# Ordering the second block's mixer steps by modelled engine times, with the convolution's taps as filler

## The reference

```python
z_conv, z_cq, z_ckv, z_kr, z_four = split_mixing(u @ w_in[l])
k_lat, v_lat = mla_kv(z_ckv, z_kr, ...)       # 8 heads, 64 + 32 wide keys, 64 wide values
q_lat = mla_q(z_cq, ...)
attn = attend_blocked(q_lat, concat(k_ctx, k_lat), concat(v_ctx, v_lat))
y = merge_branches(u, conv_module(z_conv, ...),  # 31 taps over time on 384 channels, layer norm, silu, w_pw
                   attn @ w_o_mla[l],
                   fourier_mix(z_four, ...),      # 4 groups: 2-D Fourier transform, then w_fourier
                   w_bgate[l], b_bgate[l], w_out[l])
# merge: (g0 * y_conv + g1 * y_mla + g2 * y_four) @ w_out, g = sigmoid(u @ w_bg + b)
```

## Time and profile before

| | |
|---|---|
| median of 3 runs | 2709.94 us (2701.28 to 2718.32) |
| profiled run: time, span | 2710.06 us, 2708.2 us |
| mean granted TensorE clock | 0.986 |
| TensorE busy | 2613.0 us (96%) |
| VectorE busy | 1691.8 us (62%) |
| ScalarE busy | 1084.0 us (40%) |
| HBM read | 377.40 MB, 140 GB/s |

### The profile page before, as it was taken

How to read it: one execution, slowest core, us unless ns; L and a number is a source line. 1 busy time by engine, 2 the same in 40 slices (tenths; PEclk the granted TensorE clock), 3 DMA queues, 4 the chain that set the end, 5 groups by cost and what they waited for, 6 DMA issues and landing times.

```text
span 2708.2 us, 38912 instructions
## 1 busy us (share of the span) xinstructions
PE 2613.0 (96%) x15924; PEld 2313.5 (85%) x15924; DVE 1691.8 (62%) x2681; ACT 1084.0 (40%) x1686; POOL 69.9 (3%) x64
## 2 busy tenths in 40 slices
PE   7999898999999999999999999999999999998998
PEld 7998788999888888778888888889888888888998
DVE  6767554677767655656644677655555456776664
ACT  5546633545322223344243422224222224555543
POOL 0001032000000000000010000000000000000000
PEclk9999899999999999999999999999999999999999
DMA  7764200566455543112323355543443433234454
GB/s 263 237 229 174 80 9 32 172 233 211 149 191 180 181 146 109 55 37 70 100 86 102 119 191 172 181 161 118 140 140 131 136 102 122 74 131 158 166 194 147
DMA packets 110114, 381.00 MB, mean 141 GB/s; under 512 B 12016, under 2 KB 17392, under 8 KB 109552
## 3 DMA queue, kind: packets, MB, share of 16 engines
q1 hardware_dynamic: 108928, 373.32, 41.3%
q10 hardware_dynamic: 1008, 5.18, 0.5%
HBM read 377.40 MB, written 1.05 MB: 140 GB/s over the span
## 4 chain that ended last, share of the span: by engine, by line
PE 88%; DVE 6%; ACT 4%; issue 2%; DMA 0%; ACTq 0%; DVEq 0%
PE B L1458 25%; PE B L1459 25%; PE B L1460 25%; ACT w_hi L1779 2%; DVE w_lo L2075 2%; PE B L1718 1%; PE B L1701 1%; PE B L1473 1%; PE B L1611 1%; PE B L1474 1%; PE B L1475 1%; PE B L1625 1%; PE B L1708 1%; PE B L1618 1%; DVE AC L2321 1%
## 5 line engine op out<-in xcount | busy, mean ns | idle before, releaser
L1458 PE MATMUL B<-U,w_hi 128*128 128x256 f32 (+1 forms) x2896 | 963.4, 333 | 9.5 <-DVE w_lo L2075 5.5
L1459 PE MATMUL B<-U,w_hi 128*128 128x256 f32 (+1 forms) x2896 | 953.9, 329 | 0.0
L1460 PE MATMUL B<-U,w_lo 128*128 128x256 f32 (+1 forms) x2896 | 953.7, 329 | 0.0
L2075 DVE TENSOR_TENSOR w_lo<-w_raw,w_hi 128x1024 fp32r<-128x1024 f32 (+3 forms) x587 | 684.6, 1178 | 418.1 <-ACT w_hi L1779 417.3
L1779 ACT ACTIVATE w_hi<-w_raw 128x1024 fp32r<-128x1024 f32 (+3 forms) x587 | 591.1, 1012 | 507.1 <-PE B L1460 484.1
L1458 PEld LDWEIGHTS B<-U,w_hi 128*128 128x128 f32 x2896 | 548.8, 189 | 66.5 <-issue 11.1
L1459 PEld LDWEIGHTS B<-U,w_hi 128*128 128x128 f32 x2896 | 547.1, 189 | 53.3 <-issue 2.2
L1460 PEld LDWEIGHTS B<-U,w_lo 128*128 128x128 f32 x2896 | 546.7, 189 | 51.5
L1458 PE MATMUL B<-HHf,w_hi 128*128 128x256 f32 (+1 forms) x1122 | 364.3, 325 | 1.8 <-DVE w_lo L2075 1.8
L1460 PE MATMUL B<-HHf,w_lo 128*128 128x256 f32 (+1 forms) x1122 | 363.6, 324 | 0.0
L1459 PE MATMUL B<-HLf,w_hi 128*128 128x256 f32 (+1 forms) x1122 | 363.6, 324 | 0.0
(11 more groups left out here) (351 smaller groups left out, 2628.9 us busy)
## 6 DMA issues: line engine op xcount, KB each, us to landing
w_raw<-in_w SPq DMA_DIRECT2D x504, 512.0 KB, 4.2
w_ada<-in_w SPq DMA_DIRECT2D x144, 512.0 KB, 3.4
w_raw<-in_w SPq DMA_DIRECT2D x58, 384.0 KB, 3.1
w_raw<-in_w SPq DMA_DIRECT2D x16, 240.0 KB, 2.5
X<-in_x SPq DMA_DIRECT2D x2, 1024.0 KB, 9.7
w_raw<-in_w SPq DMA_DIRECT2D x8, 256.0 KB, 2.7
BW<-in_bias ACTq DMA_DIRECT2D x1, 1536.0 KB, 10.2
K<-in_consts ACTq DMA_DIRECT2D x2, 640.0 KB, 5.7
```

The source lines that it names most:

```text
L1458: pe.matmul(o, hi, xh, start=i == 0 and s.start, stop=False)
L1459: pe.matmul(o, hi, xl, start=False, stop=False)
L1460: e = pe.matmul(o, lo, xh, start=False, stop=i == last and s.stop)
L2075: dve.tensor_tensor(w_lo[:, plan.slot[u], 0:n], w_raw[:, plan.ring[u], 0:n], w_hi[:, plan.slot[u], 0:n].bitcast(F32), ALU.subtract).then_i ...
```

## The change

`paced` gets three things: engine names in lower case take the engine's time but don't delay the task's own next step; a generator `spare` is drawn from while VectorE's clock is more than 150 ns behind TensorE's; and if nothing is due and nothing can start, time jumps ahead.

```diff
-def paced(tasks):
+def paced(tasks, spare=iter(())):
     free, later, ready = dict(P=0, A=0, D=0), list(tasks), {}
     while later or ready:
+        while free["D"] + HOP < free["P"] and (ns := next(spare, 0)):
+            free["D"] += ns
         for g in [*sorted((g for g in ready if ready[g] <= free["P"]), key=ready.get), *later]:
...
         else:
-            free["P"] = min(t for t in ready.values() if t > free["P"])
+            free["P"] = min([t for t in ready.values() if t > free["P"]], default=max(free.values()) + 1000)
             continue
...
             for engine, ns in took:
-                t = free[engine] = max(t, free[engine]) + ns
-                t += HOP
+                end = free[engine.upper()] = max(t, free[engine.upper()]) + ns
+                if engine.isupper():
+                    t = end + HOP
```

```diff
+        P = lambda k, n_=n: ("P", round(k * n_ * 1.328))
+        split = lambda c=1024: (("a", 150 + c), ("d", 150 + c))
+        A, Dv = (lambda n_=n, m=1: ("A", m * (200 + round(0.8 * n_)))), (lambda n_=n, m=1: ("D", m * (150 + round(1.05 * n_))))
         def taps():
-            left, turn = [(i, c) for i in range(1, 31) for c in range(3)], 0
-            while left:
-                turn += 1
-                k = pace[-1] * turn // 2 - pace[-1] * (turn - 1) // 2
-                self.add("taps", key=l, n=n, arg=tuple(left[:k]))
-                left = left[k:]
+            for i in range(1, 31):
+                for c in range(3):
+                    self.add("taps", key=l, n=n, arg=((i, c),))
+                    yield 180 + round(1.15 * n)
+            tapped.append(l)
+        def layer_norm():
+            while not tapped:
                 yield
...
latent:
-                yield
+                yield *split(), P(8, nn), ("d", 400 + 3 * nn), ("a", 400 + 2 * nn)
prep:
-                yield
+            yield *split(480), P(3), Dv(), P(2, 512), Dv(512)
...
+            yield ("P", 800 * ns), Dv(m=3)
soft:
-                yield
+            yield P(2, nk), Dv(nk), ("D", 150), Dv(nk), ("D", 150), A(nk), A(nk)
...
+            yield ("P", 275 * nk // 64), A(nk)
...
+            yield ("P", 140 * nk // 64),
...
fourier:
-                while not l and len(prepared) < 2 * j + 1:
-                    yield
...
+            yield *split(), P(8), A()
...
+            yield ("P", 1520 * ns), Dv(512)
...
+            yield ("P", 3040 * ns),
branch:
-                yield
+                yield *split(), P(8)
...
-                yield
+                yield *split(128 * nk), P(nk)
layer norm:
+            yield Dv(m=5), A(), A()
...
+            yield P(4), A(), A()
...
+                yield Dv(), A(), Dv()
...
-        beside(main(), taps())
+        fours, spare = set(), taps()
+        tasks = [front()]
+        for h in range(8):
+            tasks += [prep(h), *(soft(h, s) for s in range(ns))]
+            if h % 2 == 0:
+                tasks.append(fourier(h // 2))
+        if l:
+            tasks = tasks[:1] + [fourier(j) for j in range(4)] + [g for i, g in enumerate(tasks) if i and (i - 1) % 5 != 2]
+        paced([*tasks, heads_out()] + ([beside_heads()] if l else []), spare)
+        self.add("rows", need=(("pv", (l, 7, ns - 1)),))
+        if not l:
+            paced([branch(2, "FO", "wf", 4, four, alone)], spare)
+        paced([layer_norm(), last()], spare)
```

More of the change, by code:

```diff
@@ L907, in rope, with front @@
             TM.done(t, ("rope", key))
-        prepared, todo, krt = {}, {}, set()
-        def attention():
+        prepared, todo, krt, roots, outs = {}, {}, set(), [], set()
+        def front():
             gq, gk = [], []
@@ L958, in soft @@
[L958 to L975, removed]
-                yield
[L977 to L991, removed]
-                PS.done(b, ("soft_o", (l, h, s)))
-                for sm, t in work:
-                    SM.done(sm, ("soft_o", (l, h, s)))
@@ L996, in attention, with prep @@
-            tasks = []
-            for h in range(8):
-                tasks.append(prep(h))
-                tasks += [soft(h, s) for s in range(ns)]
-            yield from rounds(tasks, WIDTH)
+            yield *split(), P(8, 512), Dv()
+            roots.extend((rq, rk))
+        def prep(h):
+            while not roots:
+                yield
+            rq, rk = roots
+            yield from QR.room()
+            yield from KR.room()
+            yield from PS.room(3)
+            q, kk = QR.get(), KR.get()
+            wts = self.weights([(f"wuq{l}", k, 96 * h, 96) for k in range(3)] +
+                               [(f"wkn{l}", k, 96 * h, 96) for k in range(2)])
+            b = self.gemm(("q", l, h), None, n, m=96, x=f"CQ{l}", wts=wts[:3],
+                          need=tuple(("lat_lo", ("cq", l, k)) for k in range(3)))
+            self.add("q_in", key=(l, h), n=n, b=b, q=q, rb=rq, need=(old,))
+            PS.done(b, ("q_in", (l, h)))
+            b = self.gemm(("k", l, h), None, 512, m=96, x=f"CK{l}", wts=wts[3:],
+                          need=tuple(("lat_lo", ("ck", l, k)) for k in range(2)))
+            self.add("k_in", key=(l, h), b=b, kk=kk, rb=rk, need=(old,), arg=kk.i not in krt)
+            krt.add(kk.i)
+            PS.done(b, ("k_in", (l, h)))
+            yield *split(480), P(3), Dv(), P(2, 512), Dv(512)
+            yield from PS.room(2)
+            yield from TM.room()
+            rope((l, h), q, n)
+            yield ("P", 800 * ns), Dv(m=3)
+            todo[h] = ns
+            prepared[h] = (q, kk)
@@ L1001, in attention, with heads_out @@
+        def heads_out():
+            while len(outs) < 8 * ns:
+                yield
             banks = []
@@ new lines, in fourier @@
+        def fourier(j):
+            yield from PS.room()
+            yield from TM.room()
+            b = self.gemm(("fz", l, j), win(1440 + 128 * j), n)
+            t = TM.get()
+            self.add("four_z", key=(l, j), n=n, b=b, t=t)
+            PS.done(b, ("four_z", (l, j)))
+            yield *split(), P(8), A()
+            half = []
+            for s in range(ns):
+                yield from AR.room()
+                yield from PS.room()
+                b, q = PS.get(), AR.get()
+                self.add("four_1", key=(l, j, s), b=b, t=t, q=q, need=(old,))
+                PS.done(b, ("four_a", (l, j, s)))
+                half.append(q)
+            TM.done(t, ("four_1", (l, j, ns - 1)))
+            yield ("P", 1520 * ns), Dv(512)
+            yield from PS.room()
+            b = PS.get()
+            for s, q in enumerate(half):
+                self.add("four_2", key=(l, j, s), b=b, q=q)
+                AR.done(q, ("four_2", (l, j, s)))
+            self.add("four_o", key=(l, j), n=n, b=b, need=(old,))
+            PS.done(b, ("fo_lo", (l, j)))
+            yield ("P", 3040 * ns),
+            fours.add(j)
@@ L1064, in mix2, with beside_heads, last @@
         alone = () if l else (("four_2", (l, 3, ns - 1)), ("pv", (l, 7, ns - 1)))
-        def in_turn(*gens):
-            for g in gens:
-                yield from g
-        def main():
-            if l:
-                yield from rounds((in_turn(fouriers(), branch(2, "FO", "wf", 4, four, alone, 1)), attention()), 2)
-                self.add("rows", need=(("pv", (l, 7, ns - 1)),))
-            else:
-                yield from rounds((fouriers(), attention()), 2)
-                self.add("rows", need=(("pv", (l, 7, ns - 1)),))
-                pace.append(LATE)
-                yield from branch(2, "FO", "wf", 4, four, alone)
+        def beside_heads():
+            while len(fours) < 4:
+                yield
+            yield from branch(2, "FO", "wf", 4, four, alone, 1)
+        def last():
             yield from branch(1, "AT", "wo", 4, att, alone)
```

96 lines of the change are left out of this document (41 added, 55 removed).

## The result

The changed kernel takes 2719.08 us (median of 20 runs, 2713.5 to 2729.09), the kernel before 2705.53 us in the same comparison (20 runs, 2698.95 to 2718.32). The ratio is 1.0048, 95% interval 1.0035 to 1.006: about 13 us slower. The forecast was 2701 us. The profiled execution of the changed kernel has a span of 2714.9 us and a mean granted clock of 0.986, as before. Lines of the code lie 18 further down: a tap is L2339, a score matmul L1719, a transpose L1726, `w_lo` L2093.

The account below looks back on a forecast made before the run. TensorE was taken to bound the kernel, busy 2613.0 of 2708.2 us, with at most 24.7 us to win. Terms -3 - 3.6 - 3 + 1 = -8.6 us gave 2701 us from 2710, range 2686 to 2725.

Parts of the forecast that it names:

- rival B: Both layers' heads: planner overfills VectorE with 23.6 us of taps before splits and evacuations; slower, up to 2725 us; 17%.
- the three signs: PE waiting for w_lo behind five or more taps; layer 0's heads idle above 6 us; conv branch stall 4 us or more.
- taps in layer 0: Layer 0: about the same number of taps as before stay after the heads, where nothing waits; 0 us.
- on average VectorE has room: Argument against overfilling: VectorE busy 139 of 180 us in layer 0, 102 of 134 in layer 1; only bursts hurt.
- Layer 0's heads, -3 us: Layer 0's heads: a Fourier tile's work fills the wait before the first scores; -3 us, 30% of the 10.2 us bound.
- The 4.0 us that I put down to the clock: Layer 0's first scores: twelve matmuls took 7.88 us, should take 3.87 at the full clock; 4.0 us lost.
- Taps in layer 1, -3.6 us: Layer 1: some 15 taps instead of 33 after the heads, so the wait for w_lo goes; -3.6 us.
- The conv branch, -3 us: Layer 1's layer norm and conv branch: due times win half of the 6.1 us from stall and clock; -3 us.
- Tables in layer 1's heads, +1 us: Layer 1's heads: gates fall more finely among softmaxes; two or three more table-load pairs delay exponentials; +1 us.
- rival A: Nothing changes: the waits go and others of like size take their place; 2705 to 2715 us; 20%.

Follow-up runs that it names:

- the kernel with short draws: The changed kernel, except that the planner may put in at most 2 taps at a time; ratio 1.0028 to the kernel before.
- the mended kernel: The changed kernel, with taps right behind a Fourier tile's or the attention output's evacuation moved ahead of it in both layers' heads; ratio 0.9963 to the kernel before.

## Why the prediction was wrong, point by point

**Direction and size.** I forecast 9 us less and measured 13 us more, inside the range's upper part. I gave a loss of more than a few us to rival B and to its mechanism, 17%; the sign of the likeliest case was wrong. That nothing would move by more than 1% came true, but two of the three signs that I had named for being wrong came too: idle above 6 us in layer 0's heads (11.0) and a wait for `w_lo` behind a run of more than five taps (ten, though just behind the heads). The third, a stall of 4 us at the conv branch, came in two parts.

**The step that failed is the one on taps in layer 0,** "nothing waits there: 0", together with the argument against B that "on average VectorE has room", 139 of 180 us. Room on average is true and says nothing: VectorE's free time stood *ahead* of its evacuations and the taps behind them. I had even written that Fourier's second half leaves room in the model, and had not asked on which side of `four_o` a tap drawn at that moment lands in the list. Only 20 taps came after the heads (I expected about the same 44), so 24 more went ahead, into the heads (59 taps between 1121 and 1264 us; the kernel before has 34 up to 1260). Eight of these stand in one solid run behind `four_o`; ten of the 20 form the other, behind `at_out`. These two runs cost 2.25, 2.36 and 2.78 us of waits and, with the clock, most of the 12.2 us by which the mixer is shorter with the taps moved (418.8 against 406.6); runs of five behind the other tiles were moved too.

**B was half right.** I said that it "decides once taps leave less than a unit's time before its split", and at 1273 us that is what happened. But its price, 23.6 us out of PE times that are too long, comes from one of two errors. With the place mended, long times cost nothing measurable (0.9963 with them, 0.9967 without). With the place left wrong, they are worth most of the loss (1.0048 with them, 1.0005 without). So the loss needs taps behind evacuations, and PE's long times make it large. That they do it by the length of the runs is likely and not shown: the kernel with short draws, at 1.0028, kept the eight taps behind `four_o` in one piece. B looked for taps "in front of splits and evacuations", not behind the latter.

The trace has 110 to 123 ns for a transpose in a row of twelve (1.32 us, and 1.47 in the mended kernel), and the planner uses 275. The Trainium skill (TensorE: Matmul & The Clock Gate, Part 4: PE-mode transpose) gives about 275 ns for one inside a kernel. Which of the two the planner believes didn't matter once the taps stood ahead.

**Layer 0's heads, -3 us,** was right as a term for the order of the heads alone. The wait for the first query is gone and the clock at the first scores is 1.00; the three waits of PE's transposes behind `soft_o` are gone. With the taps moved the mixer takes 3.5 us less than before (410.1 - 406.6), and PE's idle time falls from 6.15 to 3.3 us. Three Fourier tiles, not the two that I had counted, are evacuated by the time of the first scores (at 1106, 1137 and 1158 us; the scores start at 1156.84), and this cost nothing either way. The 4.0 us that I put down to the clock at the old kernel's first scores are somewhat too many: those twelve matmuls are eight of 512 columns and four of 256, while the eight that took 2.58 us are four of each. The granted clock gives 3.4 us (0.58 over the eight us from 1136).

**Taps in layer 1, -3.6 us.** Just after the heads the waits for `w_lo` fell from 3.6 us in 24 to 1.3 us in 25, and VectorE is no longer full; the taps there are 22 in place of 33, a little over the 20 that I had named:

```profile
2390.00:2415.00 25.00, 23.69 (x200) 23.32 (x199) 21.25 (x40) 11.74 (x18) 0.00 (x0) 1.00 0.58 187
2415.00:2450.00 35.00, 30.11 (x235) 29.27 (x234) 18.19 (x28) 22.63 (x33) 4.59 (x6) 0.95 0.42 142
```

**The conv branch, -3 us, was not there.** The stall of 4.4 us put down to "issue" went, and 4.6 us in two waits for `w_lo` came (1.69 and 2.86 us, at 2429 and 2441), the clock at 0.95. ScalarE's timeline shows the likely cause, the old one in a new place: ln_out's silu and the gates' sigmoid still alternate, each with its table. Before the second wait ScalarE itself waits 2.0 us for VectorE's part of ln_out. No run tests this:

```profile
2425.08 1.28 ACT L2047 ACT_TABLE_LOAD   x1
2426.38 0.51 ACT L2047 ACTIVATE AC<-AC,PC 128x256 f32<-128x256 f32 x1
...
2427.24 1.99 ACT L1797 ACTIVATE w_hi<-w_raw 128x1024 fp32r<-128x1024 f32 x2
2429.25 1.28 ACT L2064 ACT_TABLE_LOAD   x1
2430.55 0.48 ACT L2064 ACTIVATE TMP<-B,PC 128x256 f32<-128x256 f32 x1
2431.04 1.28 ACT L2047 ACT_TABLE_LOAD   x1
...
2436.27 0.51 ACT L2047 ACTIVATE AC<-AC,PC 128x256 f32<-128x256 f32 x1 [2.02 <-DVE AC L2359]
...
2437.25 1.28 ACT L2064 ACT_TABLE_LOAD   x1
```

The function starts right after its 1.28 us load here too (2425.08 and 2426.38). The Trainium skill (ScalarE: Activation LUTs, What ACT_TABLE_LOAD costs) gives about 2.66 us for a switch, with a drain. That drain doesn't show in these rows.

I took half of a gain on the ground that due times might help, though I had read that the model has no table load. The lower bound, zero, was the better reading.

**Tables in layer 1's heads, +1 us, had the wrong sign.** In these heads the loads went from 9 (2305 to 2396 us) to 1 (2315 to 2390), not up. Gates did not "fall more finely among the softmaxes": none falls there at all. Before, gates of branch 2 ran at 2316, 2330, 2347 and 2369 us, between exponentials; after, the first table for a gate is loaded when the last exponential is done:

```profile
2374.03 0.69 ACT L2019 ACTIVATE TMP<-B,SMALL 128x512 f32<-128x512 f32 x1
...
2376.19 1.28 ACT L2064 ACT_TABLE_LOAD   x1
```

The planner starts the next task of the list when none is due, and `beside_heads` is the last of the list; that this is why it came so late is read from the code. Branch 2, which had covered the heads, stands behind them, so the stretches just after the heads compared above do not hold the same steps. Over the whole kernel the loads in front of exp, sigmoid and silu went from 20 + 12 + 4 to 16 + 6 + 4:

```profile
L1776 ACT ACT_TABLE_LOAD x16 | 20.5, 1283 | 1.0 <-PEq L2631 0.7
L2064 ACT ACT_TABLE_LOAD x6 | 7.7, 1283 | 0.1
...
L2047 ACT ACT_TABLE_LOAD x4 | 5.1, 1283 | 0.1
```

PE's waits for ScalarE in layer 1's heads (1.4 and 1.0 us) went too, and 3.1 us of waits for VectorE's rotated queries and their neighbours took their place: rival A's pattern, in one stretch. The terms of layer 1 add up to -5.6 us in the forecast; its mixer moved by -0.3.

**What stays open.** Layer 0's mixer grew by 8.8 us. Over the whole mixer PE's idle time went from 7.2 to 12.1 us. By the granted clock in stretches of ten us, (1 - granted clock) x 10, the loss to the clock went from 3.4 to 5.1 us. That makes 6.6 us; the rest I did not assign. Outside the two mixers the changed kernel's profiled execution is 1.7 us shorter, so nothing else was lost there. The medians differ by 13 us (9.5 to 16 by the interval), the two profiled executions by 6.7 and their mixers by 8.4. Single executions of the kernel before range over 19 us, but why the medians lie further apart than the mixers is open.

## What to carry to other kernels

When a planner fills an engine's free time, ask not only whether there is room but on which side of the engine's next *waiting* instruction the filler lands: each engine here works through its list in order (VectorE stood idle for 5.3 us while eight taps stood right behind the operation that it waited to do), so room that lies ahead of an evacuation can't be used from behind it. A step whose evacuation is added in the same turn as its matmuls must take filler before the evacuation; giving the evacuation a cost in the model cures the stall but pushes the filler to the end, where it can be late for the next phase. And a wait named after one producer should be followed back one step further on the producer's own timeline: here exponentials and `w_lo` were named, and solid runs of taps stood in front of both.

## What the runs showed that I had not expected

The granted clock fell after waits of 2 to 3 us, as it did after the first scores' wait: 0.76 from 1250 to 1260 us, behind waits of 2.25 and 2.36 us, and 0.83 from 1270 to 1280, around the wait of 2.78. About a quarter of what the mending of three waits gave back (2.4 of 10 us) came from the clock. A count of idle time alone leaves this out. The price isn't the same each time. Behind the same wait of 2.47 us the same twelve score matmuls took 7.88 us in the kernel before and 6.25 us in the one with only layer 1 new, whose layer 0 is in the old order (granted clock 0.58 and 0.79 over the eight us from the wait's end). And after layer 1's heads in the kernel before, three waits of 3.6 us in total, the longest 1.8, left the clock at 1.00.
